# The place of one filler matmul in five of the eight steps of a two-direction scan

## The reference

```
def step(S, inp):
    r_t, w_t, k_t, v_t, kk_t, b_t = inp
    sa = jnp.einsum('bhij,bhj->bhi', S, kk_t)
    S = S * w_t[:, :, None, :] - sa[..., None] * b_t[:, :, None, :] + v_t[..., None] * k_t[:, :, None, :]
    return S, jnp.einsum('bhij,bhj->bhi', S, r_t)
...
for d in range(N_DIR):
    s0 = jnp.zeros((B, RWKV_HEADS, RWKV_HEAD, RWKV_HEAD), jnp.float32)
    s_ctx, yc = wkv_scan(s0, *dir_inputs(tc, d), reverse=(d == 1))
    _, yx = wkv_scan(s_ctx, *dir_inputs(tx, d), reverse=(d == 1))
```

## Time and profile before

| | us |
|---|---|
| runs of the kernel (3) | 2879.65, 2882.47, 2885.64 |
| median | 2882.47 |
| the profiled execution: its time | 2887.08 |
| the profiled execution: its span | 2884.3 |
| TensorE busy in the span | 2783.5 (97%) |
| VectorE busy | 1893.8 (66%) |
| ScalarE busy | 991.5 (34%) |
| GpSimd busy | 567.4 (20%) |
| granted TensorE clock, mean | 0.981 |

### The profile page before, as it was taken

How to read it: one execution, slowest core, us unless ns; L and a number is a source line. 1 busy time by engine, 2 the same in 40 slices (tenths; PEclk the granted TensorE clock), 3 DMA queues, 4 the chain that set the end, 5 groups by cost and what they waited for, 6 DMA issues and landing times.

```text
span 2884.3 us, 66324 instructions
## 1 busy us (share of the span) xinstructions
PE 2783.5 (97%) x25890; PEld 2101.3 (73%) x25890; DVE 1893.8 (66%) x3509; ACT 991.5 (34%) x1684; POOL 567.4 (20%) x708
## 2 busy tenths in 40 slices
PE   5999999999999999999988999999899999999997
PEld 1456566666566666566655888887799999998886
DVE  2246677766677776667764656654589989995444
ACT  2232333322333322333312433333444444443332
POOL 0022332122333122233120200000023333330000
PEclk7999999999999999999989999999999999999999
DMA  9722122332222332222235455554445555554553
GB/s 388 284 91 97 55 89 96 111 111 96 63 86 89 111 111 96 77 79 89 75 121 195 141 183 188 189 189 165 170 141 180 186 178 187 177 185 154 186 180 139
DMA packets 75801, 412.84 MB, mean 143 GB/s; under 512 B 9296, under 2 KB 11984, under 8 KB 42608
## 3 DMA queue, kind: packets, MB, share of 16 engines
q1 hardware_dynamic: 74864, 408.10, 41.2%
q0 software_dynamic: 768, 2.10, 0.2%
HBM read 405.38 MB, written 4.19 MB: 142 GB/s over the span
## 4 chain that ended last, share of the span: by engine, by line
PE 91%; DVE 4%; DMA 2%; ACT 1%; issue 1%; SPq 0%; DVEq 0%; ACTq 0%; PEldq 0%
PE PB L723 21%; PE Q L992 13%; PE Q L987 7%; PE PB L987 4%; PE PB L982 4%; PE CH L987 3%; PE PB L983 3%; PE CH L983 3%; PE CH L982 3%; PE Q L859 3%; PE Q L845 3%; PE Q L866 2%; DMA ring<-w_mod_dram 2%; PE CH L900 2%; PE CH L930 1%; PE CH L920 1%
## 5 line engine op out<-in xcount | busy, mean ns | idle before, releaser
L723 PE MATMUL PB<-hT,ring 128*128 128x512 f32 (+1 forms) x1536 | 664.5, 550 | 1.5
L1721 DVE TENSOR_TENSOR w_lo_r<-ring,w_hi_r 128x1536 fp32r<-128x1536 f32 (+3 forms) x178 | 390.0, 2191 | 203.8 <-ACT w_hi_r L1307 203.8
L1307 ACT ACTIVATE w_hi_r<-ring 128x2048 fp32r<-128x2048 f32 (+2 forms) x178 | 325.8, 1830 | 313.6 <-PE PB L987 104.3
L723 PEld LDWEIGHTS PB<-hT,ring 128*128 128x128 f32 x1536 | 258.6, 189 | 126.3 <-issue 83.2
L1265 ACT ACTIVATE arena<-CH 128x64 f32<-128x64 f32 x128 | 28.6, 223 | 512.9 <-PE CH L903 324.3
L983 PE MATMUL PB<-hT_r,w_hi_r 128*128 128x256 f32 x832 | 204.7, 286 | 0.0
L1896 DVE TENSOR_TENSOR w_lo_r<-ring,w_hi_r 128x1408 fp32r<-128x1408 f32 x62 | 100.7, 1625 | 134.4 <-ACT w_hi_r L1426 134.4
L2007 POOL TENSOR_TENSOR w_lo_r<-ring,w_hi_r 128x512 fp32r<-128x512 f32 x88 | 118.1, 1342 | 357.1 <-ACT w_hi_r L1307 357.1
L1576 DVE SCALAR_TENSOR_TENSOR arena<-ring,csilp,arena 128x512 f32<-128x512 f32 x240 | 180.7, 753 | 5.9 <-DMA ring<-w_mod_dram 1.3
L992 PE MATMUL Q<-ff_r,w_hi_r 128*128 128x512 f32 x704 | 176.7, 399 | 3.5 <-ACT w_hi_r L1426 3.5
L982 PE MATMUL PB<-hT_r,w_hi_r 128*128 128x256 f32 x704 | 175.9, 289 | 2.8 <-DVE hT_r L1823 2.8
(11 more groups left out here) (268 smaller groups left out, 5337.0 us busy)
## 6 DMA issues: line engine op xcount, KB each, us to landing
ring<-w_up_dram SPq DMA_DIRECT2D x88, 1024.0 KB, 4.9
ring<-w_mod_dram SPq DMA_DIRECT2D x128, 512.0 KB, 3.7
ring<-w_rkv_dram SPq DMA_DIRECT2D x48, 1024.0 KB, 5.9
ring<-w_down_dram SPq DMA_DIRECT2D x64, 704.0 KB, 4.0
ring<-w_mod_dram SPq DMA_DIRECT2D x32, 1024.0 KB, 9.1
ring<-w_ga_dram SPq DMA_DIRECT2D x16, 1024.0 KB, 4.9
ring<-w_gb_dram SPq DMA_DIRECT2D x16, 1024.0 KB, 4.9
ring<-w_pa_dram SPq DMA_DIRECT2D x16, 1024.0 KB, 4.8
```

The source lines that it names most:

```text
L723: last = mm(PB[slot % 2][:, 0:cols], tile(n, kt), hT[:, kt, 0:cols], start=(kt == 0), stop=(kt == KT - 1))
L1307: f(w_hi_r[:, r % 2, 0:n], ring[:, r, 0:n], ACT.Copy).then_inc(hi_rdy, 1)
L1721: tt(w_lo_r[:, r, 0:n], ring[:, r, 0:n], as_f32(w_hi_r[:, r % 2, 0:n]), ALU.subtract).then_inc(lo_rdy, 1)
```

## The change

In steps 0 to 4 of pairs 0 to 13 filler A moves from behind the right sides to ahead of them, where it has stood in steps 5 to 7 already. The work is the same. `last.then_inc(rhs_ps[d], 1)` is the signal to the two copies.

```
                 for s in range(NCH):
                     if more >= 1 and 1 <= s <= 6:
                         project(i + 1, 2, s + 9, s + 10)
-                    if more == 2 and s >= 5:
+                    if more == 2:
                         project(i + 2, 0, 2 * s, 2 * s + 1)
                     for d in range(2):
                         ch = chunk_at(d, s)
...
                         last.then_inc(rhs_ps[d], 1)
                     if s >= 5:
                         outputs(s - 1)
-                    elif more == 2:
-                        project(i + 2, 0, 2 * s, 2 * s + 1)
                     if more == 0:
                         gv_part(0, PB, 24 + s, 25 + s)
```

## The result

| | before | after |
|---|---|---|
| runs | 4 | 4 |
| median, us | 2884.05 | 2904.76 |
| all runs, us | 2879.65 to 2887.63 | 2901.39 to 2905.81 |
| the profiled execution, us | 2887.08 | 2901.39 |
| its span, us | 2884.3 | 2899.5 |

The account below looks back on a forecast made before the run. TensorE's list was taken to bound the kernel. Steps 1 to 4 (+0.35 - 0.20 = +0.15 us each, 56 steps, +8.4 us) plus step 0 (+6.7 us) gave +15.1 us on 2882.5: 2897.6 us, range 2885 to 2908.

Parts of the forecast that it names:

- the likeliest case: Whole kernel: 15.1 us slower, 2897.6 us, with its own range of 2888 to 2903.5; chance 0.70.
- rival 4: Steps 1 to 4: the switch saving does not come, or step 1 waits at the state too; 2909 to 2913 us, chance 0.08.
- What bounds the kernel: Pairs: TensorE works 85.22 of 85.74 us, so time added to its list or waits opened there go straight to the end.
- The saved switch, 0.20 us: Steps 1 to 4: V and A in one row return to small matmuls once, saving 0.20 us a step, 11.2 us in all.
- The uncovered copy, 0.35 us: Steps 1 to 4: solutions wait for the right sides' copy; 0.22 late plus 0.13 slower, 0.35 us a step.
- Step 0, +0.48 us: Step 0: last inverse level to solutions takes 2.76 us instead of 2.28, +0.48 a pair, +6.7 us in all.
- inverse level alone 0.98: Step 0: the last inverse level before filler A takes 0.98 us, one term of the 2.76 us sum.
- Even that slow case is covered, by 0.20: Step 1's state link: B covers VectorE's 1.28 us products, 2.45 against 2.25 us; otherwise some 0.3 us x 14 = 4 us.
- if L928 waits for L1653: Sign of being wrong: the state link (L928) waits for VectorE's L1653; no idle time at L928 was forecast.
- no cancelling: Rival that the effects nearly cancel: +0.02 a step, +0.31 in step 0, 5.4 us, 2887.9 us in all; chance 0.13.
- no gain: Rival that copies are quick enough and the saved switch decides: faster, 2871 us, or 2878 with step 0's cost; chance 0.04.
- no fall of the clock: Rival that new waits lower TensorE's clock in each pair: some 2.7 us a pair, 38 us, near 2935 us; chance 0.05.

## Why the prediction was right, and where its sizes were off

The time, 2904.76 us, is inside the range of 2885 to 2908, but above the 2888 to 2903.5 that the likeliest case had for itself. It is inside because the range had been widened for part of rival 4 and for medians that differ by themselves (that of before moved by 1.6 us). The 15.1 us of the sum are below the interval of the measured difference, 16.7 to 23.9 us.

**What bounds the kernel**: right. The times of the pairs, +1.45 us x 14 = 20.3, agree with the timed 20.5, so nothing took back more than the width of the interval.

**The saved switch, 0.20 us**: right. The row of two fillers took 1.91 in the changed kernel and in three of the experiments.

**The uncovered copy, 0.35 us**: right. Solutions came 0.89 after the right sides (0.88 forecast) and the steps took 4.75 us (4.74). It had been read from a single step of pair 14, and that step was a true sample of the order to come.

**Step 0, +0.48 us**: 0.56 measured. The term "inverse level alone 0.98" was mis-sized: it is the distance from L859 to another small matmul, and to a filler it is 853.41 - 852.33 = 1.08. The trace of before had a row for it, another level (L845) with fillers behind it, 839.05 - 837.98 = 1.07:

```profile
837.98 1.15 PE L845 MATMUL Q<-arena,woven 64*64 64x64 f32 x32
...
839.05 2.84 PE L723 MATMUL PB<-hT,ring 128*128 128x512 f32 x6
```

The rest (A 1.06, right sides to solutions 0.70 against 0.72) held. Together the two make the 0.08 that was missing, 14 x 0.08 = 1.1 us.

**"Even that slow case is covered, by 0.20"**: this is the step that failed. It was also one of the prediction's own signs of being wrong, "if L928 waits for L1653", and in step 1 L928 does (for L1651, which is that line in the changed kernel). I had taken 1.28 us for the two decay products from pair 14 as a slow case. In the changed kernel they took 1.69 to 1.70 in each of the 14 pairs, in the one with A ahead in step 1 alone 2.27, in the one with A ahead in step 0 alone 2.55, and the state link waited. The consequence that the prediction had priced, "step 1 alone would pay some 0.3 us x 14 = 4 us", is what happened: 0.24 x 14 = 3.4 us. It stood in a sentence and in the second half of rival 4, which had a chance of 0.08 with its first half, and should have been in the sum. That the total is still near is no merit of this step. With both corrections the forecast would have been 15.1 + 1.1 + 3.4 = 19.6 us, against 20.3 by the pairs and 20.5 timed; the rest is the 0.01 a step between 0.15 and 0.16.

**The rivals**: no cancelling (the lower bound of 0.22 for the exposure was wrong, since B follows 0.51 after the solutions instead of 0.38), no gain, no fall of the clock. The granted clock was 1.00 from 200 to 1450 us in both kernels; behind that it fell in both.

## What to carry to other kernels

A filler between dependent small matmuls earns what it hides, less what it costs to come back from it; both can be read off the profile as distances from start to start, if somewhere in the kernel the link stands bare. Here that is 0.36 to 0.52 us against 0.20, so joining fillers loses. With other small independent work as the cover it came out even or a little ahead (4.51 us a step instead of 4.59, but 4.71 in step 1).

When work is moved in time, the partners that do not move set new waits: VectorE's two short products were harmless where they fell before, and held up a link 0.2 to 0.8 us once they met GpSimd at another point, in the kernels that moved A in steps 0 and 1. A price read from one meeting of the two is not a bound. And parts that wait for the same fixed event do not add: test a change's parts singly and the whole.

## What the runs showed of the hardware

Short VectorE instructions from SBUF to SBUF (128x64) did not get done while GpSimd ran a multiply. Two of them took 0.41 us with GpSimd idle, and 0.74, 1.28, 1.70, 2.27, 2.34 and 2.55 beside it. VectorE's copy out of PSUM just ahead of them was not held up: 0.22 us beside a multiply (859.45 in the changed kernel) and 0.23 with GpSimd idle (864.44).

How long the two take depends on the boundary between multiplies that they meet. The first gets done when the running multiply ends. What happens to the second goes by which starts first, it or the next multiply. The second product alone and the next multiply, pair 7, before:

```profile
848.17 0.24 DVE L1650 TENSOR_SCALAR arena<-arena 128x64 f32<-128x64 f32 x1
848.25 1.28 POOL L1932 TENSOR_TENSOR arena<-arena 64x512 f32<-64x512 f32 x1
```

The same in the changed kernel.

```profile
859.98 1.26 POOL L1931 TENSOR_TENSOR arena<-arena 64x512 f32<-64x512 f32 x1
859.99 1.30 DVE L1648 TENSOR_SCALAR arena<-arena 128x64 f32<-128x64 f32 x1
```

Before, the second product starts 0.08 us ahead of the multiply and passes; in the changed kernel it starts 0.01 behind it and waits for all of it. So it is in all of pairs 0 to 13 of both kernels, in pair 14 of before (1448.44 against 1448.52, it passes), and in the kernels with A ahead in step 0 or in step 1 alone (it waits, 2.55 and 2.27 us). The two boundaries differ by a gap: L1932 starts 0.06 after the end of L1933, but L1933 (L1931 after) 0.03 to 0.04 before the recorded end of L1932 (L1930 after). Where that gap comes from stays open.

The Trainium skill (SBUF — State Buffer, "SBUF: two separate sides") calls the SBUF port pair that VectorE and GpSimd share an exclusive lock, held by whichever instruction starts first for all its time, with the other engine fully blocked; of VectorE's instructions those in a 2-port mode take part. These rows agree on who waits; no run here shows which mode the decay products ran in. That the two modulation products took 3.33 us in the kernel with the late multiplies agrees with its line that a VectorE instruction with two SBUF inputs contends as well.

Independent small matmuls of the two links ran among each other: sixteen records of right sides and eight of solutions took 0.68 us when nothing ordered them (the kernel without the wait), where the two links in turn, with a filler between them, take 0.66 + 0.38 = 1.04.
